# Two transformer stacks on one core: where tile pairs begin in the convolution projections, the maximum as one operation, and a new deal of modulation tiles

## The reference

```python
def masked_softmax(s, mask):
    s = jnp.where(mask, s, NEG_INF)
    m = jnp.max(s, axis=-1, keepdims=True)
    p = jnp.where(mask, jnp.exp(s - m), 0.0)
    return p / jnp.maximum(jnp.sum(p, axis=-1, keepdims=True), TINY)

def conv_ffn(h, w_up, conv_w, conv_b, w_down):
    S = h.shape[1]
    a = h @ w_up
    pad = jnp.pad(a, ((0, 0), (CONV_W - 1, 0), (0, 0)))
    y = conv_b
    for j in range(CONV_W):
        y = y + conv_w[j] * pad[:, j:j + S, :]
    gate, val = jnp.split(y, 2, axis=-1)
    return (jax.nn.silu(gate) * val) @ w_down

    for i in range(DEPTH_2):                       # second_block
        mod = c_act @ ada_w[i] + ada_b[i]
        sh1, sc1, g1, sh2, sc2, g2 = jnp.split(mod, 6, axis=-1)
```

## Time and profile before

| | us |
|---|---|
| median of 3 runs | 2406.55 |
| lowest, highest | 2406.28, 2409.95 |
| the profiled execution | 2407.11 |
| its span | 2405.2 |
| TensorE busy in the span | 2342.6 |
| VectorE busy | 1771.6 |
| ScalarE busy | 556.5 |

### The profile page before, as it was taken

One profiled execution on the slowest core, in us unless ns is written; L12 is line 12 of the kernel. 1 busy time (PEld: TensorE's weight loads), 2 busy tenths in 40 slices (PEclk: granted clock), 3 DMA queues, 4 the chain that ended last, 5 costly groups with the idle time before them and its releaser, 6 DMA issues.

```text
span 2405.2 us, 44464 instructions
## 1 busy us (share of the span) xinstructions
PE 2342.6 (97%) x17384; PEld 2074.4 (86%) x17384; DVE 1771.6 (74%) x3724; ACT 556.5 (23%) x1432; POOL 182.2 (8%) x287
## 2 busy tenths in 40 slices
PE   8999999999999999999999999999999999999998
PEld 4477999654679998999999699999789998899998
DVE  5876888457858986787996569977958986666883
ACT  2232010025421102202221322212223212202220
POOL 0000001000000010001100011111001100001100
PEclk9999999999999999999999999999999999999999
DMA  6434777741337776557867278674348866446752
GB/s 250 145 119 141 245 250 265 261 143 36 111 112 271 255 264 224 195 220 228 257 210 278 69 225 252 225 272 158 114 146 268 254 241 200 157 150 184 210 175 81
DMA packets 134860, 472.78 MB, mean 197 GB/s; under 512 B 15120, under 2 KB 17296, under 8 KB 134160
## 3 DMA queue, kind: packets, MB, share of 16 engines
q1 hardware_dynamic: 95136, 339.22, 40.4%
q0 software_dynamic: 39536, 130.89, 18.2%
HBM read 469.01 MB, written 1.05 MB: 195 GB/s over the span
## 4 chain that ended last, share of the span: by engine, by line
PE 84%; DVE 9%; DMA 3%; issue 3%; ACT 2%; DVEq 0%; SPq 0%; ACTq 0%
PE pair L643 50%; PE bank L643 32%; DMA adat<-adaw_dram 2%; DVE att_s L2116 1%; DVE arena L2111 1%; DVE arena L1939 1%; DVE rstd L1826 1%; DVE h L1829 1%; DVE arena L1945 1%; PE bank L927 1%; PE bank L1033 0%; DMA ring<-stream_dram 0%; DVE adat L2302 0%; ACT h L1448 0%; DVE arena L1941 0%
## 5 line engine op out<-in xcount | busy, mean ns | idle before, releaser
L643 PEld LDWEIGHTS bank<-arena 128*128 128x128 f32 (+2 forms) x3288 | 363.6, 186 | 45.4 <-issue 25.8
L643 PE MATMUL bank<-arena 128*128 128x128 f32 (+3 forms) x3288 | 391.7, 280 | 9.8 <-ACT arena L1484 4.9
L643 PE MATMUL pair<-arena,ring 128*128 128x128 f32 (+1 forms) x2726 | 376.3, 295 | 6.3 <-issue 3.8
L643 PEld LDWEIGHTS pair<-arena,ring 128*128 128x128 f32 x2726 | 349.7, 192 | 22.6 <-issue 6.1
L643 PE MATMUL pair<-arena 128*128 128x128 f32 (+6 forms) x2970 | 351.8, 282 | 5.8 <-DVE arena L1945 3.4
L643 PE MATMUL pair<-h,ring 128*128 128x128 f32 (+1 forms) x2224 | 340.8, 309 | 7.0 <-issue 3.4
L643 PEld LDWEIGHTS pair<-arena 128*128 128x128 f32 (+3 forms) x2970 | 315.6, 186 | 34.0 <-issue 23.5
L643 PEld LDWEIGHTS pair<-h,ring 128*128 128x128 f32 x2224 | 310.9, 191 | 25.9 <-issue 4.1
L643 PE MATMUL bank<-arena,ring 128*128 128x128 f32 x2550 | 306.6, 276 | 3.4 <-DVE arena L2169 2.5
L643 PEld LDWEIGHTS bank<-arena,ring 128*128 128x128 f32 x2550 | 295.6, 192 | 5.7 <-DVE arena L2169 2.8
L2302 DVE CUSTOM_DVE_ANT_0 adat<-adat,crow,cols 128x1024 f32<-128x1024 f32 x192 | 243.2, 1280 | 59.0 <-DMA adat<-adaw_dram 59.0
(11 more groups left out here) (268 smaller groups left out, 2532.3 us busy)
## 6 DMA issues: line engine op xcount, KB each, us to landing
ring<-stream_dram SPq DMA_DIRECT2D x638, 512.0 KB, 4.8
adat<-adaw_dram POOLq DMA_DIRECT2D x192, 512.0 KB, 5.0
ring<-stream_dram POOLq DMA_DIRECT2D x73, 256.0 KB, 6.1
arena<-gmrows_dram POOLq DMA_DIRECT2D x2, 2560.0 KB, 12.1
arena<-cmpw_dram POOLq DMA_DIRECT2D x1, 2112.0 KB, 9.9
x<-x_in_dram SPq DMA_DIRECT2D x2, 512.0 KB, 4.4
arena<-mem_in_dram SPq DMA_DIRECT2D x1, 1024.0 KB, 9.1
arena<-gmws_dram POOLq DMA_DIRECT2D x2, 512.0 KB, 14.2
```

What stands on the lines that cost most here:

```text
L643: return nc.tensor.matmul(out, lhsT, rhs, start=start, stop=stop)
```

## The change

- `SEVEN`: pairs are rows 1 to 20 in all four convolution projections. Before, they were 2 to 20 without 11 in the first three and 2 to 20 in the last.
- In `whole_row(0)` the moving sums and the weight sums of pair 1 come ahead of the taps of row 0; those of pair 2 stand behind them.
- Tables of tiles: `ADA_UP` (new, for up0 and up1: 24 tiles in each where there were 22, rows 4, 9 and 14 have two, row 21 none), `ADA_CONV` (now per layer: rows 1, 8 and 20 one more than the odd rows' one, and row 14 in the first), `ADA_NSA` 12 for 8, `ADA_DOWN` 12 for 13 in another order, `ADA_GMO` (new, for gm_out0: 6 for 13). In `up_tiles`, rows that make no weight sums take their tile behind the gate.
- `maxima` of a masked unit with 256 keys becomes one fused operation for each head: out = -(score + mask) * scale with a running minimum, which is the negated maximum. exp reads the negated values with scale -1.

```diff
-SEVEN = {f"cup{i}": [t for t in range(2, 21) if t != 11] for i in range(LAYERS2 - 1)}
-SEVEN[f"cup{LAYERS2 - 1}"] = range(2, 21)
-ADA_CONV = [(t % 2 == 1 and t < FT - 1) + (t in (11, 20)) for t in range(FT)]
-ADA_NSA = {0: 1, 1: 2, 2: 2, 4: 2, 6: 1}
+SEVEN = {f"cup{i}": range(1, 21) for i in range(LAYERS2)}
+ADA_CONV = [[(t % 2 == 1 and t < FT - 1) + (t in (1, 8, 20)) + (i == 0 and t == 14) for t in range(FT)]
+            for i in range(LAYERS2)]
+ADA_NSA = {0: 2, 1: 2, 2: 3, 4: 3, 6: 2}
-ADA_DOWN = (2, 1, 1, 2, 1, 1, 2, 2, 1)
-ADA_FFN = FT + sum(ADA_DOWN)
+ADA_DOWN = (1, 1, 1, 1, 1, 2, 2, 2, 1)
+ADA_GMO = (1, 1, 0, 1, 1, 0, 1, 1, 0)
+ADA_UP = [(t < FT - 1) + (t in (4, 9, 14)) for t in range(FT)]
+ADA_FFN = sum(ADA_UP) + sum(ADA_DOWN)
...
+        def fused(un):
+            return un["mask"] is not None and un["nk"] == TOK
...
                         ins = nc.scalar.activation(p, p, ACT.Exp, bias=att_s[:, u % 3, 0, e:e + 1],
+                                                   scale=-1.0 if fused(un) else 1.0,
                                                    accum_out=att_s[:, u % 3, 1, e:e + 1])
...
+                    if fused(un):
+                        for e in range(2):
+                            ins = V.tensor_tensor_reduce(out=p[:, e, :], in0=s[:, e, :], in1=un["mask"],
+                                                         scale=-un["scale"], scalar=3e38, op0=ALU.add, op1=ALU.min,
+                                                         accum_out=att_s[:, u % 3, 0, e:e + 1])
+                        ins.then_inc(sem("scores_read"), 1)
+                        V.engine_nop().then_inc(sem("max_done"), 1)
+                        return
...
                     if q is not None:
                         after(total)
                         less = chained(weight_sum(base, DK // 2, own, 1))
-                    ada_tile()
-                    if q is not None:
+                        for _ in range(ADA_UP[t]):
+                            ada_tile()
                         after(less)
                         weight_sum(base, DK // 2, own, 3).then_inc(sem("up_summed"), 1)
                     if t >= 2:
                         gated(t - 1)
+                    for _ in range(0 if q is not None else ADA_UP[t]):
+                        ada_tile()
...
                 def whole_row(t, ada):
                     q = None
+                    if t == 0:
+                        dve.wait_ge(sem("h_done"), H_DONE[f"ffn2_{i}"] + TT * DK)
+                        moving_sums(h, upT[1], 0, DK // 2)
+                        q = next_pair()
+                        added_twins(q, added_first(q))
+                        q = None
...
                     if t == 0:
-                        dve.wait_ge(sem("h_done"), H_DONE[f"ffn2_{i}"] + TT * DK)
-                        moving_sums(h, upT[1], 0, DK // 2)
                         q = next_pair()
                         added_twins(q, added_first(q))
...
-                        residual(f"gm_out{i}", f"ffn2_{i}", gain, gate, ada_tiles(ADA_DOWN) if i == 0 else None, high)
+                        residual(f"gm_out{i}", f"ffn2_{i}", gain, gate, ada_tiles(ADA_GMO) if i == 0 else None, high)
```

6 lines of the change are left out of this document (3 added, 3 removed).

## The result

| | before | after |
|---|---|---|
| median, us | 2406.69 (4 runs, 2406.28 to 2409.95) | 2387.68 (4 runs, 2384.84 to 2392.80) |
| profiled span | 2405.2 | 2386.4 |
| TensorE busy | 2342.6 | 2336.7 |
| VectorE busy | 1771.6 | 1773.0 |

The ratio is 0.992, with a 95% interval of 0.9901 to 0.994: 19.0 us faster, forecast 2385.6. One profiled execution further down, the first of the kernel with the load at row 17, took 8436 us with the same instructions and is left aside.

The account below looks back on a forecast made before the run. TensorE, busy 97% of the span, was taken as the bound. Gains of 4.6 (pairs), 9.4 (tiles) and 7.5 (maximum) sum to 21.5 us, from 2407.1 to 2385.6; range 2377 to 2397.

Parts of the forecast that it names:

- the fused pair: Sign of being right, masked 256-key units: the fused pair of operations takes 0.8 us to the next one, formerly 1.33.
- Under 1 us: Sign of being right: TensorE's list of waits without L1945 and L1874, or with under 1 us of both.
- rival 3: Convolution projections: VectorE's debt misses its margin after row 8 and at the start, 0.3 to 1 us each; 2388, chance 0.08.
- Seven pairs, 4.6: Convolution projections: seven rows become pairs, each saving 0.66 us of TensorE; 4.6 us, range 3.5 to 4.6.
- at the start: Pair 1 of a convolution projection: its sums finish before TensorE asks for them, cover 0.5 us, costed at nothing.
- in the middle: Row 8 of a convolution projection: VectorE runs 2.58 us late where 2.7 passes, and rows 9 to 15 pay it back.
- Rival 4: Convolution projections: VectorE becomes the bound, average row over 6.25 us, slower than before; 2415 at 0.5 over, chance 0.03.
- The deal, 9.4: New deal of tiles: waits removed in down residuals and gm_out0, 7.4 us, and in up projections, 2.0 us.
- the residual term: Down residuals and gm_out0: 5.3 us of L1945's waits and all of two others go; 7.4 us, bounds 4.5 and 8.5.
- Rival 2: Down residuals: tiles still late, pair 1 keeps four, 0.4 to 0.8 us per residual stays; 2389, chance 0.12.
- The maximum, 7.5: Fused maximum in 28 masked units: 4.5 us in NSA, 2.0 in first attention, 1.0 in MLA and tails; range 3 to 11.
- rival 1: Masked attention units: the maximum costs what it did, operations without overlap, some 1 us of 7.5 left; 2392, chance 0.11.

Follow-up runs that it names:

- the load at row 17: Changed kernel with the fourth layer's 3 MB bulk load asked for at row 17 of the third convolution projection, not row 3: 2383.64 us, repeated 2383.98.

## Why the prediction was right, point by point

**What bounds the kernel.** TensorE does, and its list of waits named the places: of the entries in the earlier trace rows, 16.8 us together, 3.3 are left. Of the signs that the prediction named, the fused pair at 0.71 us and the first down pairs without a wait came out. "Under 1 us" for L1945 and L1874 was missed at 1.1, 0.6 of it behind the stop, and was met with the load at row 17 (0.5). The banks' release as TensorE's releaser inside a projection, a sign of rival 3, showed once, in the third projection.

**Seven pairs, 4.6.** Measured 4.9 alone; 1.4 for each projection with two new rows and 0.82 for the last, which is 0.66 a row and 0.1 to 0.15 a projection for the small wait on row 0's banks. It held at the start: the sums took 4.61 us (4.51 said) from 1094.16 to 1098.77, and TensorE asked for the weight sums at 1098.98, a cover of 0.2 where 0.5 was said. (By the prediction's own rows TensorE ends row 0 at 1168.76 - 56.91 = 1111.85, not 1111.7, which would have made it 0.6.) It held in the middle: 2.58 of 2.7 used, which is 0.17 between release and use. Rival 3 was a near miss, and the run with two tiles at row 8 shows what it would have been.

**What failed in this part** is the sentence on traffic: "There are 7 more of 256 KB in all, nothing beside 473 MB". The total was right (474.64 MB for 472.78) and no measure of anything. The added weights share a queue with a load of 3 MB, in one of the four projections, and the extra set of weights and the tile at row 1 stood ahead of it. VectorE's wait for them, 1.7 us in the kernel before and so hidden, became 5.9 against a slack of 2.5. I had looked for the first accumulating DMA of a projection and not at the others. Rival 4 named the mechanism ("the added sums can wait for their DMA"), but as something that decides over an average row. It needs one row only. Cost: 5.8 us, which no term had: 3.39 of stop, 1.7 of clock and 0.73 in the down projection behind.

**The deal, 9.4.** 9.5 by medians, 11.3 by stages. With the 0.68 of its stop put back the stages give 12.0: 1.1 from each of the two up projections, for 1.0, and 9.8 from the residuals, for 7.4 and an upper bound of 8.5. The waits that the residual term counted did go as said: of the 5.8 us on L1945 all but the 0.55 in the HGRN2 stage, which is the 5.3 taken, and the other two whole. What was too small is the size: the nine stops are 7.3 us as idle time and 8.9 from start to start, since each is some 0.15 longer than its idle figure, and 0.9 more lies in smaller intervals that I haven't broken down. On the other side, the profile of the kernel before had larger stops in the five down residuals than the two others with that code, by 0.5 and 1.8 us, so the 12.0 may be high; the medians, over 22 and 7 runs, agree with the 9.4.

In the up projections I had ScalarE's SiLU of the last row late next by 0.2 to 0.3. The merged view shows no gap at the end of up0:

```profile
369.09 7.18 PE L648 MATMUL bank<-arena,ring 128*128 128x128 f32 x59
...
371.04 0.99 DVE L2183 TENSOR_TENSOR arena<-arena 128x256 f32<-128x256 f32 x2
```

59 matmuls up to the end of that view, where the kernel before stood for 1.23 us after 20. From start to start two small intervals are left, 0.19 and 0.10 us over the usual 0.11. The size was right, the reason wrong: in both kernels TensorE's matmul there starts 0.06 us behind the end of the first of the two gates, that of row 20 (1.4 us of loss before, with 374.58 for the gate and 374.64 for the matmul; now 371.45 and 371.51). The SiLU of the last row (to 371.57) and the last row's gate (to 372.03) end behind that and aren't waited for at that matmul.

Of the mechanism in the down residuals the runs show the outline: putting the fourth tile of pair 0 back cost 1.1 us in one profile, with that of pair 1 3.2 in another. Rival 2 named pair 1's four tiles as the danger; in the kernel after, with three in pair 0, they did no harm.

**The maximum, 7.5.** 6.3 alone by medians; by stages of the kernel after 4.75 in NSA (4.5 said), 1.83 in the first attention (2.0), 0.52 in MLA, 7.1 in all. The gain per unit was 0.62, above the 0.48 taken and near its upper bound of 0.6 (time by columns alone would be twice 0.30 and 0.05 for the signal, a gain of 0.68). It made no difference to the sum because TensorE's own idle time was the cap, as the prediction argued from the earlier trace rows, and the run with all masked units fused shows that cap. The rule of the Trainium skill (VectorE: DVE Perf Modes, "Rules for kernel authors" and "The DRAIN you can't avoid"), by which only the number of operations counts and the time would by rival 1's rows have been 2392, loses: the second fused operation starts 0.35 us after a first that lasts 0.42, and the maximum alone gave 6.3 us. The second of these sections itself excepts a next operation that isn't held (held is its word for one that starts only when all earlier ones have finished); the prediction had left that out.

**The sum.** 21.5 forecast. The terms as the stages show them, without the stop, are 5.2 (1.44 + 1.48 + 1.42 + 0.85 for the four projections), 12.0 and 7.1, 24.3, near the 24.0 by which the span with the load at row 17 is shorter. From that the collision took 5.8, and some 18.7 is left. By medians the three parts alone give 4.9, 9.5 and 6.3, 20.7, with stops of 0.60 and 0.68 in two of them; the load at row 17 gives 24.8 and 24.6. Each of these is known to some 3 us, so they don't contradict the stages. That the forecast was only 2 us off is luck in part: an error of 2 or 3 us one way met one of 5.8 the other way. Each alone lay within the range.

## What to carry to other kernels

A small transfer with a deadline can be held up by a bulk load on its queue, however small its share of the traffic: look for each queue at what stands ahead of the urgent transfer in its worst row, and try the bulk behind the last of them, which gave back 5.8 us here. Slack is worth a sum of its own, row by row: it is spent only once, by whatever comes first, and what is hidden today (1.7 us here) adds to tomorrow's 1.2 and 1.4 before anything shows. Time taken from an engine counts up to the point where the next bound stands, and behind it a further saving of the same kind was worth nothing here. And a stage's difference between two profiles is only as good as the stage is steady: compare kernels that share its code first.
